# Twelve of twenty filler blocks as seven-product pairs ahead of a gated-DeltaNet recurrence

## The chip, the cores and the metric

The kernel runs on one core of one Trainium2 chip. The metric is the device time of one execution in microseconds. The engines are TensorE (PE in the profile), VectorE (DVE), ScalarE (ACT), GpSimd (POOL) and SyncE (SP), which issues most DMAs. They run side by side, each in its own order, and wait for each other on semaphores.

## The reference

One block of a streaming encoder on x of 1024 frames by 1024 channels, all float32:

```
proj = x @ w_in                      # 4872 columns: attention q/k/v, DeltaNet q/k/v,
                                     # beta, decay, output gate z, two branch gates
A = banded attention with rotary and sinks (chunks of 64 frames, window 2 chunks)
q, k, v = silu(causal_conv4(dqkv)); q, k l2-normalized
# chunked gated delta rule, per head (4 heads of 128), chunk of 64:
m_low = strict_lower((k*beta) k^T * decay);  t_inv = inverse(I + m_low)
u = t_inv (v*beta);  w = t_inv (k*beta*exp(g));  a = (q k^T) * decay
v_new = u - w state;  o = (q*exp(g)) state + a v_new
state = state*exp(g_last) + (k*exp(g_last - g))^T v_new        # scan over chunks
B = rmsnorm(o) * silu(z)
y = sigmoid(gateA) * (A @ wbA) + sigmoid(gateB) * (B @ wbB)
x = LN(alpha*x + y @ w_out);  x = LN(alpha*x + relu(x @ w_up)^2 @ w_down)
```

The change touches the input projection, the recurrence and their order, and no formula.

## The kernel before, in words

Every large product of two float32 matrices is made of three matmuls on operands split into a high and a low part (hi*hi, hi*lo, lo*hi), each 128 by 128 by 512 columns. The input projection has 37 blocks of 128 output columns. A plain block is 2 halves of 512 frames x 8 contraction tiles x 3 = 48 such matmuls. Two blocks taken together can be made with seven products of half size instead of eight (the scheme of Strassen and Winograd, `in7`, L2040): 7 x 4 x 3 = 84 matmuls for two blocks instead of 96. POOL makes the sums of the weights (`in_sums`), ACT the high parts (`in_hi`) and copies of partial results (`in_snap`), DVE the low parts (`in_lo`) and the additions (`combine_in`).

Block 0 is made plainly, blocks 1 to 16 in `N_IP = 8` pairs, and the last 20 blocks (4 of z, 16 of gates) plainly. The first of these 20 is made directly behind the pairs. The other 19 are **fillers**: PE puts their matmuls (L2118) one by one between the small products of the recurrence, in numbers written out by hand. Their weights come through two ring slots, split by POOL (`split_ring`, L774 and L777). A finished half block is copied out by ACT (`evac_half`, L980) and stored to DRAM (`park`), from where it is read back.

The recurrence goes over 8 tiles of 128 frames (two chunks each), all four heads at once. It is pipelined by hand: step t works on **t**, the scan and the attention of tile t; on **a** = t+1, the inverse of that tile's triangular matrix (five levels `a_y`, `a_u`, PE and DVE in turn, L2185, L1567, L1573, L1578); and on **n** = t+2, transposes, norms and decays of that tile (`a_grow`, `a_trk`, `a_trq`, `a_trv`, `a_d`, `a_norm`, `a_kd`, `a_vb`, `a_ee`). The functions named `step` of PE, DVE and ACT give each engine's order. For tile t and chunk c the scan is `b_ks` (state read, L2243), `b_x` (DVE), `b_vn` (product with the inverse, L2253), ACT's copy to `vn`, `b_ds` (state product, L2263), `b_state` (DVE). The attention is `b_scores`, `b_max`, `b_exps`, `b_prob`, `b_pt`, `b_pv`. The output is `b_o`, `b_osq` (squares on ACT), `b_on` (DVE: twelve small dependent operations for an inverse root, then two scalings), `b_ont`, `b_yd`. `a_norm` holds a second root of the same kind for q and k. Small DVE operations in `chain` wait each for the one before.

POOL makes the rotary products of tile t+1 once the second score product of tile t is done (`rope`), and one or two weight splits per step. SP loads each tile's data a step or more ahead. Steps -2 and -1 fill the pipeline; PE's numbers of fillers per place are

```
full = [12, 2, 6, 0, 3, 12, 0, 1, 0, 11, 2, 9, 11, 2, 11, 0, 2, 4, 1]   # then the rest up to 96
```

for the steps of tiles 0 to 6, so 96 fillers (two blocks) per step, and 96 in tile 7's step. Behind the recurrence come the branch projections (L2370), w_out, and the FFN.

Of the kernel before, what the change touches and what calls it, by code (L numbers as in the profile page):

```python
# [29 lines left out]
ALU = mybir.AluOpType  # L30
# [26 lines left out]
N_STD = 3  # L57
PIECES = ("A11", "A12", "S3", "A22", "S1", "S2", "S4")
# [12 lines left out]
N_IP = 8  # L71
# [58 lines left out]
def hybrid_block(nc, A, out):  # L130
    with ExitStack() as ctx:
# [53 lines left out]
        vn = workb("vn", 512, [P, NH, P])  # L185
# [23 lines left out]
        dqs = worka("dqs", 512, [P, NH, P])  # L209
        dd, eml, emu, em0 = [worka(name, 256, [P, NH, CH]) for name in ("dd", "eml", "emu", "em0")]  # L210
# [289 lines left out]
        def _(sp):  # L500
# [21 lines left out]
            def load_dv(t):  # L522
                sp.dma_start(dv[:, :, :], park[2 * NH:3 * NH, :, bass.ds(PAD + t * P, P)].rearrange("b p s -> p b s")).then_inc(dv_in, 16)
# [8 lines left out]
            def load_qk(t):  # L532

                if isinstance(t, int) and t == 0:
                    for h in range(2):
                        sp.wait_ge(ub_out[h], 16 * (B_DZ - N_DN))
# [82 lines left out]
            load_v(NT - 1)
            load_dz(NT - 1)  # L620
# [145 lines left out]
        def _(pool):  # L766
# [120 lines left out]
        def _(act):  # L887
# [53 lines left out]
            def in_snap(n, i):  # L941
# [59 lines left out]
            for n in range(N_IP):  # L1001
# [6 lines left out]
                if n == N_IP - 1:  # L1008
# [10 lines left out]
                if n == N_IP - 1:  # L1019
# [12 lines left out]
            in_snap(N_IP - 1, 3)  # L1032
            store_pair(N_IP - 1)
            act.sem_inc(uni_out, 4 * N_IP)
# [4 lines left out]
            for h in range(2):  # L1039
                evac_half(B_DZ, h, 2 * (B_DZ % 2) + h, ACT.Silu)  # L1040
# [55 lines left out]
            def b_vn(t, c):  # L1096
                act.wait_ge(vn_mm, 2 * t + (c + 1))
                r = slice(c * CH, (c + 1) * CH)
                cp(vn[r, :, :], (C0h, C1h)[c][r]).then_inc(vn_ok, 1)
# [8 lines left out]
            def step(t, a, n, p, fill):  # L1108

                if a is not None: a_t1(a, p)  # L1110
                if t is not None: b_vn(t, 0)
                if t is not None: b_exps(t, 0)
                if t is not None: b_pt(t, 0)
                fill(0)
                if t is not None: b_ya(t, 0)
                if t is not None: b_vn(t, 1)
                if n is not None: a_scalars(n, 1 - p)
# [1443 lines left out]
```

## Time and profile before

| | |
|---|---|
| time, median of 3 runs | 1417.92 us (1417.14 to 1417.92) |
| the profiled execution | span 1415.8 us from its first to its last instruction; some 2 us lie around it |
| PE busy | 1401.8 us (99%) |
| DVE, ACT, POOL busy | 978.8, 577.9, 277.7 us |
| pairs (blocks 1 to 16) | to 188.0 us |
| block 17, steps -2 and -1 | 188.0 to 251.4 us |
| steps of tiles 0 to 6 | 251.4 to 570.1 us |
| step of tile 7 | 570.1 to 605.9 us |

The profile gives each instruction's start and duration, and for idle time of an engine the instruction that ended it. Matmuls are pipelined: a row's duration overlaps the next one's, so the cost of one is the distance between starts.

### The profile page before, as it was taken

Reading aid. Unit: us, or ns where it says so; the run is one execution under the profiler, and the core shown is the slowest. Engines: PE = TensorE matmul, PEld = TensorE weight load, DVE = VectorE, ACT = ScalarE, POOL = GpSimd, SP = SyncE. Lnnn points to the kernel's source line nnn. Section 1 sums busy time; section 2 is a strip of 40 time slices with the busy share of each in tenths; the row PEclk is TensorE's granted clock in tenths of the full one; section 3 lists DMA queues with packets and bytes.
Section 4 is the critical chain, followed back from the end, with each engine's and each line's share of the span. In section 5 each row is a group of like instructions: output and inputs, shape, how many; then the busy total and the mean of one; then the engine's idle time right before and its main releaser. Section 6 shows DMA issues by size and latency. Waiting matters only on the chain.

```text
span 1415.8 us, 22360 instructions
## 1 busy us (share of the span) xinstructions
PE 1401.8 (99%) x8502; PEld 1154.4 (82%) x8502; DVE 978.8 (69%) x1792; ACT 577.9 (41%) x1258; POOL 277.7 (20%) x301
## 2 busy tenths in 40 slices
PE   9999999999999999999999999999999999999997
PEld 8788887888888888778888888888888888888885
DVE  7999844666666665364528797666674777777778
ACT  5655532323332332342203355555544544444540
POOL 4332234423333243323910000000000000000002
PEclk9999999999999999999999999999999999999999
DMA  6233362443244422234442144433345875555422
GB/s 212 90 119 114 109 194 86 122 119 105 75 114 113 120 64 88 72 113 161 166 176 90 60 165 162 164 147 131 137 158 192 324 238 180 163 165 187 126 69 119
DMA packets 114134, 195.01 MB, mean 138 GB/s; under 512 B 27696, under 2 KB 59632, under 8 KB 111728
## 3 DMA queue, kind: packets, MB, share of 16 engines
q1 hardware_dynamic: 105104, 174.21, 37.2%
q10 hardware_dynamic: 8928, 19.40, 3.6%
q8 instruction: 68, 1.11, 0.3%
q14 instruction: 34, 0.28, 0.1%
HBM read 135.84 MB, written 57.74 MB: 137 GB/s over the span
## 4 chain that ended last, share of the span: by engine, by line
PE 93%; DVE 5%; DMA 1%; issue 1%; SPq 0%; ACT 0%; ACTq 0%; DVEq 0%
PE ps L2118 16%; PE ps L2495 6%; PE ps L2493 6%; PE ps L2494 6%; PE ps L2476 6%; PE ps L2477 6%; PE ps L2478 6%; PE ps L2185 4%; PE ps L2003 4%; PE ps L2004 4%; PE ps L2005 4%; PE ps L2063 3%; PE ps L2065 3%; PE ps L2064 3%; PE ps L2374 2%; PE ps L2370 2%
## 5 line engine op out<-in xcount | busy, mean ns | idle before, releaser
L2493 PE MATMUL ps<-thi,shi 128*128 128x512 f32 x416 | 161.8, 389 | 0.0
L2494 PE MATMUL ps<-tlow,shi 128*128 128x512 f32 x416 | 161.8, 389 | 0.0
L2495 PE MATMUL ps<-thi,slow 128*128 128x512 f32 x416 | 161.8, 389 | 0.0
L878 POOL TENSOR_TENSOR zt<-zt,ln2gb 128x256 f32<-128x256 f32 x4 | 3.4, 851 | 691.6 <-ACT zt L1329 691.6
L2118 PE MATMUL ps<-xh,ring2l 128*128 128x512 f32 x304 | 124.5, 410 | 0.0
L2118 PE MATMUL ps<-xl,ring2h 128*128 128x512 f32 x304 | 123.6, 407 | 0.0
L2118 PE MATMUL ps<-xh,ring2h 128*128 128x512 f32 x304 | 122.3, 402 | 0.0
L888 ACT ACTIVATE thi<-b 128x512 fp32r<-128x512 f32 x104 | 65.5, 630 | 106.5 <-PE ps L2495 106.0
L1887 DVE TENSOR_TENSOR tlow<-b,thi 128x512 fp32r<-128x512 f32 x104 | 71.8, 690 | 51.8 <-ACT thi L888 51.7
L2494 PEld LDWEIGHTS ps<-tlow,shi 128*128 128x128 f32 x416 | 78.1, 188 | 16.3
L2495 PEld LDWEIGHTS ps<-thi,slow 128*128 128x128 f32 x416 | 78.1, 188 | 16.2
L2493 PEld LDWEIGHTS ps<-thi,shi 128*128 128x128 f32 x416 | 78.1, 188 | 16.1
L777 POOL TENSOR_TENSOR ring2l<-raw,ring2h 128x256 fp32r<-128x256 f32 x112 | 89.6, 831 | 2.2
L1880 DVE TENSOR_TENSOR slow<-sraw,shi 128x512 fp32r<-128x512 f32 x104 | 71.3, 686 | 22.5 <-ACT shi L888 21.7
L888 ACT ACTIVATE shi<-sraw 128x512 fp32r<-128x512 f32 x104 | 65.0, 625 | 33.5 <-DMA zt<-xpark 17.6
L774 POOL CAST ring2h<-raw 128x1024 fp32r<-128x1024 f32 x28 | 31.3, 1117 | 228.1 <-PE ps L2118 138.2
L2118 PEld LDWEIGHTS ps<-xl,ring2h 128*128 128x128 f32 x304 | 57.1, 188 | 12.3 <-issue 0.6
L2118 PEld LDWEIGHTS ps<-xh,ring2l 128*128 128x128 f32 x304 | 57.1, 188 | 12.0 <-issue 0.6
L2118 PEld LDWEIGHTS ps<-xh,ring2h 128*128 128x128 f32 x304 | 57.2, 188 | 11.4 <-issue 0.2
L1397 DVE SCALAR_TENSOR_TENSOR cacc<-cb,convw,cacc 128x1024 f32<-128x1024 f32 x36 | 51.6, 1435 | 2.1 <-ACT cacc L959 1.3
L980 ACT ACTIVATE ub<-ps 128x512 f32<-128x512 f32 x40 | 24.0, 601 | 67.5 <-PE ps L2118 65.7
L2003 PE MATMUL ps<-slh,mg 128*128 128x512 f32 x128 | 50.0, 390 | 0.0
(442 smaller groups left out, 3636.9 us busy)
## 6 DMA issues: line engine op xcount, KB each, us to landing
raw<-in_wblk SPq DMA_DIRECT2D x55, 512.0 KB, 3.6
sraw<-hpark SPq DMA_DIRECT2D x104, 256.0 KB, 2.8
hpark<-hq SPq DMA_DIRECT2D x16, 1024.0 KB, 4.6
b<-in_wblk SPq DMA_DIRECT2D x64, 256.0 KB, 3.6
wraw<-in_wblk SPq DMA_DIRECT2D x30, 512.0 KB, 4.0
hpark<-hq SPq DMA_DIRECT2D x16, 768.0 KB, 5.0
park<-ub ACTq DMA_DIRECT2D x40, 256.0 KB, 2.1
park<-cacc ACTq DMA_DIRECT2D x12, 512.0 KB, 3.3
```

The source lines that it names most:

```text
L777: ins = pool.tensor_tensor(lo[:, k:k + 2, :], src[:, k:k + 2, :], hi[:, k:k + 2, :].bitcast(F32), ALU.subtract)
L888: cp = lambda o_, i_: act.activation(o_, i_, ACT.Copy)
L1880: tt(slow[s][:, :], sraw[s][:, :], shi[s][:, :].bitcast(F32), ALU.subtract).then_inc(lsl_ok if last else sl_ok, 1)
L1887: tt(tlow[m][:, :], src[:, :], thi[m][:, :].bitcast(F32), ALU.subtract).then_inc(ltl_ok if last else tl_ok, 1)
L2003: mm(outp, lh, rh, start=start, stop=False)
L2118: ins = mm(ps[h][:, :], w, x_, start=(r == 0), stop=(r == 23))
L2476: mm(outp, hi[:, k, :], bh_, start=first, stop=False, skip_group_check=True)
L2477: mm(outp, hi[:, k, :], bl_, start=False, stop=False, skip_group_check=True)
L2478: last = mm(outp, lo[:, k, :], bh_, start=False, stop=final, skip_group_check=True)
L2493: mm(outp, shi[s][:, ts], thi[m][:, :], start=first, stop=False, skip_group_check=True)
L2494: mm(outp, shi[s][:, ts], tlow[m][:, :], start=False, stop=False, skip_group_check=True)
L2495: return mm(outp, slow[s][:, ts], thi[m][:, :], start=False, stop=final, skip_group_check=True)
```

## The change

`N_IP` goes from 8 to 14, so blocks 1 to 28 are made in pairs; blocks 29 to 36 (`LATE` = 29 on), all gates, remain as fillers, 8 x 48 = 384 matmuls. `FILLS` says how many go to each of 31 places of each of the ten steps: 50, 35, 30, 41, 27, 31, 33, 39, 33 and 65 for steps -2 to 7. The loops over tiles are written out. Each engine's order within a step is new. The computation of the decay rates and its three small products move into the eighth and the last pair. The clearing of buffers moves behind DVE's work of step -2. `vn` becomes two buffers, each holding one chunk's rows with zeros in the other half, and the state product reads all 128 rows. POOL splits one block in steps 0, 1, 3, 4 and 6, behind the rotary work.

```diff
-N_IP = 8
+N_IP = 14
+LATE = 2 * N_IP + 1
+FILLS = [
+    [0, 0, 6, 0, 1, 0, 0, 0, 0, 0, 0, 0, 0, 1, 0, 1, 0, 2, 2, 0, 0, 0, 13, 1, 2, 0, 0, 21, 0, 0, 0],
+    [0, 0, 0, 3, 0, 3, 0, 0, 3, 0, 2, 3, 2, 1, 0, 0, 3, 0, 0, 1, 0, 3, 0, 0, 0, 0, 0, 0, 5, 1, 5],
+    [2, 1, 0, 0, 0, 2, 0, 4, 1, 0, 0, 0, 0, 0, 0, 0, 0, 0, 3, 0, 6, 0, 0, 2, 5, 0, 0, 0, 0, 4, 0],
+    [4, 2, 1, 0, 0, 2, 0, 4, 1, 0, 0, 0, 0, 0, 0, 0, 0, 0, 3, 0, 6, 0, 0, 4, 3, 0, 0, 0, 0, 11, 0],
+    [0, 0, 0, 0, 0, 2, 0, 4, 1, 0, 0, 0, 0, 0, 0, 0, 0, 0, 2, 0, 3, 0, 0, 2, 9, 0, 0, 0, 0, 4, 0],
...
+    [0, 3, 0, 0, 4, 0, 8, 0, 2, 3, 0, 3, 0, 0, 1, 1, 1, 0, 1, 10, 0, 19, 0, 0, 0, 0, 0, 9, 0, 0, 0],
+]
@@ POOL
-            split_ring(N_IP + 1, 1)
-            split_ring(10, 0)
             rope(0)
-            split_ring(10, 1)
-            split_ring(11, 0)
-            with pool.Fori(0, NT - 1) as t:
+            split_ring((LATE + 2) // 2, 1)
+            behind = {0: LATE + 3, 1: LATE + 4, 3: LATE + 5, 4: LATE + 6, 6: LATE + 7}
+            for t in range(NT - 1):
                 rope(t + 1)
-                split_ring(t + 11, 1)
-                split_ring(t + 12, 0)
+                if t in behind:
+                    split_ring(behind[t] // 2, behind[t] % 2)
@@ DVE
+            def clear():
...
+                dve.memset(st[:, :, :], 0.0).then_inc(s_ok, 1)
+                dve.memset(vn0[CH:P, :, :], 0.0)
+                dve.memset(vn1[0:CH, :, :], 0.0)
+                dve.memset(qb[:, :, :, :], 0.0).then_inc(init_ok, 1)
+            step(-2)
+            clear()
+            for s in range(-1, NT):
+                step(s)
@@ PE: state product
-                r = slice(c * CH, (c + 1) * CH)
...
-                    last = mm(C1h[:, h, :], kdec[p][r, h, :], vn[r, h, :], start=True, stop=True)
+                    last = mm(C1h[:, h, :], kdec[p][:, h, :], vnz[c][:, h, :], start=True, stop=True)
@@ PE: state read and solve
-                    if not (isinstance(t, int) and t == NT - 1):
-                        pe.wait_ge(vb_ok, t + 2)          # in b_ks, c == 0
+                    if t < NT - 1:
+                        pe.wait_ge(vb_ok, t + 2)          # in b_vn, c == 0
@@ PE: order of a step (fills between the lines left out)
+                b_ks(t, 0); b_scores(t, 0); a_kk(a); a_kq(a); b_vn(t, 0); a_t1(a); b_ds(t, 0); a_y(a, 1); b_ks(t, 1)
+                b_pt(t, 0); a_ut(a, 1); a_u(a, 1); b_vn(t, 1); a_y(a, 2); b_pv(t, 0); a_u(a, 2); a_ut(a, 2)
+                b_scores(t, 1); b_ds(t, 1); a_y(a, 3); b_o(t, 0); b_o(t, 1); a_u(a, 3); a_ut(a, 3); a_grow(n); a_y(a, 4)
+                b_pt(t, 1); a_u(a, 4); a_ut(a, 4); a_trk(n); b_ont(t); a_trq(n); a_y(a, 5); b_pv(t, 1); a_u(a, 5); a_trv(n)
+            step(-2, FILLS[0])
+            pe.wait_ge(init_ok, 1)
+            for s in range(-1, NT):
+                step(s, FILLS[s + 2])
@@ DVE: order of a step
+                b_x(t, 0); a_m(a); b_max(t, 0); a_att(a); b_state(t, 0); b_prob(t, 0); a_ys(a, 1); b_x(t, 1); a_tb(a, 1)
+                a_r(a, 1); a_ys(a, 2); a_r(a, 2); a_tb(a, 2); a_qeg(a); b_max(t, 1); a_ys(a, 3); b_state(t, 1); a_r(a, 3)
+                a_tb(a, 3); b_prob(t, 1); a_d(n); a_ys(a, 4); b_on(t); a_r(a, 4); a_tb(a, 4); a_em(n); b_yd(t); a_ys(a, 5)
+                a_kd(n); a_norm(n); a_r(a, 5); a_ee(n); a_vb(n)
```

The last two parts are shortened: in the kernel each call stands on a line with a condition that its tile exists. In ACT's new order the squares of k and q come behind the copy of a filler's first finished half; in SP's, the second weight block of a step is gone.

## Rows read from the trace of the kernel before

**Rows 1.** The page, part 1: busy time, share of the span, instructions by engine.
```profile
PE 1401.8 (99%) x8502; PEld 1154.4 (82%) x8502; DVE 978.8 (69%) x1792; ACT 577.9 (41%) x1258; POOL 277.7 (20%) x301
```

**Rows 2.** Busy us by stage: span, PE, PEld, DVE, ACT, POOL, clock, DMA.
```profile
53.00:188.02 135.02, 135.02 (x597) 111.60 (x596) 121.20 (x143) 69.67 (x100) 39.69 (x30) 1.00 0.30 110
188.02:251.40 63.38, 62.85 (x515) 50.02 (x514) 27.99 (x75) 20.05 (x58) 26.19 (x33) 1.00 0.47 146
...
297.60:343.80 46.20, 46.20 (x486) 37.60 (x485) 30.67 (x89) 14.78 (x65) 15.68 (x20) 1.00 0.37 104
```

**Rows 3.** Order of time, PE: first state product of tiles 0, 1, 7; branch projection.
```profile
251.45 1.05 PE L2243 MATMUL ps<-st,kq 128*128 128x128 f32 x8
...
297.61 1.05 PE L2243 MATMUL ps<-st,kq 128*128 128x128 f32 x8
...
570.09 1.05 PE L2243 MATMUL ps<-st,kq 128*128 128x128 f32 x8
...
605.95 0.42 PE L2370 MATMUL ps<-yh,ring2h 128*128 128x512 f32 x1
```

**Rows 4.** Order of time, PE: first product of two neighbouring pairs.
```profile
111.86 0.39 PE L2063 MATMUL ps<-xh,ipA11h 128*128 128x512 f32 x1
...
130.90 0.39 PE L2063 MATMUL ps<-xh,ipA11h 128*128 128x512 f32 x1
```

**Rows 5.** Order of time, PE, within the step of tile 1 (and just before).
```profile
296.70 0.39 PE L2118 MATMUL ps<-xh,ring2l 128*128 128x512 f32 x1
...
298.50 1.06 PE L2215 MATMUL ps<-kr,qb 128*128 128x128 f32 x8
...
303.99 0.64 PE L2185 MATMUL ps<-rinv,mm 64*64 64x64 f32 x15
304.57 0.50 PE L2118 MATMUL ps<-xh,ring2l 128*128 128x512 f32 x1
304.90 0.39 PE L2118 MATMUL ps<-xh,ring2h 128*128 128x512 f32 x1
...
305.46 1.16 PE L2263 MATMUL ps<-vn,kdec 64*128 64x128 f32 x8
306.55 0.50 PE L2118 MATMUL ps<-xh,ring2l 128*128 128x512 f32 x1
...
330.89 0.60 PE L2126 MATMUL ps<-cst,pr 128*128 128x128 f32 x4
331.33 0.60 PE L2126 MATMUL ps<-cst,dqk 128*128 128x128 f32 x4
```

**Rows 6.** Order of time, DVE, same step: beside POOL, and the output norm's root.
```profile
316.09 1.20 DVE L1589 TENSOR_SCALAR nmx<-mx 128x4 f32<-128x4 f32 x1
...
322.69 1.26 DVE L1516 TENSOR_TENSOR emu<-dd,cst 128x256 f32<-128x256 f32 x1
...
327.50 0.16 DVE L1617 SCALAR_TENSOR_TENSOR ssb<-ssb,rqs 128x4 f32<-128x4 f32 x1 [0.43 <-ACT osb L1105]
...
329.68 0.16 DVE L1620 TENSOR_TENSOR nwu<-nwu,rqs 128x4 f32<-128x4 f32 x1
```

**Rows 7.** Order of time, POOL, same step: rotary work, then a weight split.
```profile
315.99 1.27 POOL L821 TENSOR_TENSOR qsw<-qsw,cs 128x512 f32<-128x512 f32 x1
...
319.01 2.92 POOL L830 TENSOR_TENSOR qb<-qraw,qsw 64x256 f32<-64x256 f32 x4
322.35 1.32 POOL L774 CAST ring2h<-raw 128x1024 fp32r<-128x1024 f32 x1 [0.42 <-POOL qb L830]
323.75 3.34 POOL L777 TENSOR_TENSOR ring2l<-raw,ring2h 128x256 fp32r<-128x256 f32 x4
```

**Rows 8.** Order of time, ACT's queue and DVE behind the last pair.
```profile
189.64 2.24 ACTq L973 DMA_DIRECT2D park<-cb  x4
...
197.32 0.91 DVE L1501 MEMSET qb<- 128x1024 f32 x1 [4.38 <-DMA park<-cb]
198.29 0.48 DVE L1502 MEMSET st<- 128x512 f32 x1
```

More of the change, by code:

```diff
@@ L970, in store_pair @@
                 act.wait_ge(cs_ok, 4 * n + 4)
+                if 2 * n + 1 >= B_DZ and 2 * n + 1 < B_GATE:
+                    for block in range(2):
+                        c = cb[2 * (n % 2) + block][:, 3:3 + S]
+                        act.activation(c, c, ACT.Silu).then_inc(silu_ok, 1)
+                    act.wait_ge(silu_ok, N_DN + 2 * n + 3 - B_DZ)
                 for block in range(2):
@@ L1038, in _ @@
             act.activation(G[:, :, G_SDE:G_SDO + NH], G[:, :, G_SDE:G_SDO + NH], ACT.Exp).then_inc(g_dif, 1)
-            for h in range(2):
-                evac_half(B_DZ, h, 2 * (B_DZ % 2) + h, ACT.Silu)
+            in_snap(N_IP - 1, 3)
+            store_pair(N_IP - 1)
+            act.sem_inc(uni_out, 4 * N_IP)
             def a_scalars(t, p):
@@ L1106, in b_osq, with late_half, step @@
                 ins.then_inc(osq_ok, 1)
-            def step(t, a, n, p, fill):
-                if a is not None: a_t1(a, p)
+            def late_half(i):
+                b, h = LATE + i // 2, i % 2
+                evac_half(b, h, h + 2 if b == LATE else h, ACT.Copy)
+            def step(s):
+                t = s if s >= 0 else None
+                a = s + 1 if 0 <= s + 1 < NT else None
+                n = s + 2 if s + 2 < NT else None
+                p, q = s % 2, 1 - s % 2
+                first, last = sum(map(sum, FILLS[:s + 2])) // 24, sum(map(sum, FILLS[:s + 3])) // 24
@@ L1144, in _ @@
-            step(None, 0, 1, 0, z_fill)
-            for i in range(NT // 2 - 1):
-                step(2 * i, 2 * i + 1, 2 * i + 2, 1, gate_fill(2 * i))
-                step(2 * i + 1, 2 * i + 2, 2 * i + 3, 0, gate_fill(2 * i + 1))
-            step(NT - 2, NT - 1, None, 1, gate_fill(NT - 2))
-            step(NT - 1, None, None, 0, lambda i: gate_fill(NT - 1)(i) if i < 3 else None)
+                if t is not None: b_ya(t, 1)
+                for i in range(first + 1, min(last, 2 * (B_BR - LATE) - 1)):
+                    late_half(i)
@@ L1152, in _ @@
+            for s in range(-2, NT):
+                step(s)
             act.wait_ge(yd_ok, NT)
@@ new lines, in _, with fill @@
+            pe.sem_inc(uni_mm, 4 * N_IP)
+            late = {"units": 0}
+            def fill(count):
+                for _ in range(count):
+                    j, r = divmod(late["units"], 48)
+                    h, r = divmod(r, 24)
+                    k, i = divmod(r, 3)
+                    b = LATE + j
+                    s_ = b % 2
+                    if h == 0 and r == 0:
+                        pe.wait_ge(w_ready, b + 1)
+                    if r == 0 and j == 0:
+                        if h == 0:
+                            pe.wait_ge(cs_ok, 4 * (N_IP - 1) + 1)
+                        else:
+                            pe.wait_ge(snap_ok, 4 * (N_IP - 1) + 4)
+                    elif r == 0:
+                        pe.wait_ge(uni_out, 2 * b + h + 1 - (4 if j == 1 else 2))
+                    sl = slice(h * HALF, (h + 1) * HALF)
+                    w = (ring2h, ring2h, ring2l)[i][s_][:, k, :]
+                    x_ = (xh, xl, xh)[i][:, k, sl]
+                    ins = mm(ps[2 + h if j == 0 else h][:, :], w, x_, start=(r == 0), stop=(r == 23))
+                    if r == 23:
+                        ins.then_inc(uni_mm, 1)
+                    late["units"] += 1
@@ L2270, in b_o @@
                 for h in range(NH):
-                    last = mm((O0h, C0h)[c][other, h, :], att[p][r, h, :], vn[r, h, :], start=False, stop=(h == NH - 1), skip_group_check=True)
+                    last = mm((O0h, C0h)[c][other, h, :], att[p][r, h, :], vnz[c][r, h, :], start=False, stop=(h == NH - 1), skip_group_check=True)
                 last.then_inc(o_mm, 1)
```

390 lines of the change are left out of this document (171 added, 219 removed), and 4 rows, old and new, of the table FILLS.

## The prediction

> **What bounds the kernel now.** I began with the page. The tensor engine (PE) is busy 1401.8 of 1415.8 us [rows 1]. So the end is set by what PE has to do, and each instruction taken from PE is a gain as long as nothing else becomes late. The second view was the busy time by stage, with the granted clock at 1.00 of 2.4 GHz in each [rows 2]. In the seven-product pairs before the change DVE is busy 121 of 135 us, since the convolutions run there too. In one step of the recurrence (46.2 us) PE is busy throughout, DVE 30.7 us, ACT 14.8 and POOL 15.7. So DVE would have 15 us to spare in a step. The third view was PE's order of time, where a step's start can be read at the first state product: tile 0 at 251.45, tile 1 at 297.61, tile 7 at 570.09, and the branch projection begins at 605.95 [rows 3]. A pair takes 130.90 - 111.86 = 19.04 us for 84 products, 0.2267 each [rows 4]. A filler costs (297.61 - 296.70)/4 = 0.2275 us [rows 3, 5]. The busy time of 0.39 us that a row names overlaps its neighbour and isn't the cost.
>
> The profiled span is 1415.8 us, the median of the timed runs 1417.9; 2.1 us lie around the span. I sum on the trace and add the difference to 1417.9.
>
> **Stage 1, the pairs.** Six more of them: 6 x 19.04 = +114.2 us. They have no convolution from the eighth on, so DVE has room for the chain of small gate operations that moves into one of them (some 27 operations of 0.2 us). The Silu of four blocks moves to ACT there, which runs nothing long. If that cover were missing, the next pair would start late by what DVE has left over, up to 5.4 us once; I take 0. The three small gate products (0.6 us) only change place.
>
> **Stage 2, from the last pair to tile 0's first state product.** Before: 251.45 - 188.02 = 63.4 us, with 192 plain products. After: 87 fillers. I follow the order. The last sum waits for ACT's copy (0.6) and DVE's addition (0.7); then ACT issues four stores, 2.24 us [rows 8], and only then copies the scalars of tile 0. That is 4.2 us, and the 13 fillers put ahead of the row transposes fill 3.1 (13 x 0.2275, and 0.1 for the change): PE idles 1.1 us. Then 37 fillers (8.4), three more groups of transposes (331.33 - 330.89 = 0.44 each, 1.3) [rows 5] and the changes between them, to 14.8. Now the clearing of buffers sits behind DVE's last work of tile 0, no longer ahead of it: V scaled 0.7, memsets of the state 0.48 and of qb 0.91 [rows 8], and two new ones on half the partitions, which no row shows. Nearest is the state's 0.48, so 0.3 to 0.5 each; I take 0.4. PE waits for the clearing with no filler behind the last transposes: 3.3 us idle, to 18.1. Step -1 has 17 groups of 16 small products (304.57 - 303.99 = 0.58 each at most, 0.56 on average, 9.5), four of transposes (1.8), 35 fillers (8.0) and 12 changes between them (0.15, 1.8): 21.1. [rows 5] With two fillers of step 0 (0.5) and the gate products (0.6) it makes 40.3 us, -23.1. The wait for the pairs' stores, which held qb up by 4.4 us [rows 8], is met over 10 us after the stores are issued and costs nothing.
>
> **Stage 3, tiles 0 to 6.** Before: 570.09 - 251.45 = 318.6 us with 660 fillers (150.2), so 168.4 of other PE work, 24.1 per step. Now 232 fillers, 52.8 us. A filler that follows a small group starts a slower pair: 304.57 to 304.90 is 0.33, against 0.23 [rows 5]. There were 14 groups of fillers per step, now about 10: -0.7 per step. The state products on 64 rows took 306.55 - 305.46 = 1.09 us, those on 128 rows 298.50 - 297.61 = 0.89 where the same shape follows [rows 3, 5]. Widening them with zeros is worth 0 to 0.4 per step; I take 0.2, as the neighbours are mixed. So PE's floor is 168.4 - 6.3 + 52.8 = 214.9 us, 30.7 per step.
>
> DVE is now as near. Its 30.7 us hold 4.3 us in which seven operations were stretched while POOL ran: nmx took 1.20 us beside POOL's rotary products, where such small operations alone take 0.16, and emu 1.26 beside a weight split [rows 6, 7]. The row of nmx ends at 317.29, and POOL's product of qsw, begun before it, at 317.26: nmx was held until POOL let go. Add 1.1 us of gaps between dependent small operations: DVE needs 27.5 us of its own. Waits that the order can't fill, by walking through it with these durations: for the first state update 0.4, the second state read 0.5, the first tb 0.3, the second ys 1.1, together 2.3. Then POOL. Rotary work starts at each second score product, where DVE comes with mx, nmx, sdf: +1.8 as now. It runs about 7.2 us (its second product begins at 315.99, the last ends at 321.93, and the first is as long as the second) [rows 7] and meets the softmax scaling: +0.6. That makes 27.5 + 2.3 + 2.4 = 32.2 us a step for steps 2 and 5, which have no weight split. In steps 0, 3 and 4 a split of 4.4 us (cast 1.3, four subtractions) follows the rotary work directly, when DVE is in the twelve dependent operations of the output norm, which alone take 2.4 us (327.50 to 329.85) [rows 6]. Five of them can each be held to the end of a POOL instruction (+0.4 to +0.65): +2.4, so 34.6. In step 1 the split waits for its ring slot and meets less: 33.3. Step 6 prepares no further tile, which takes 6 us from DVE, so PE sets it: 29.2. Sum: 2 x 32.2 + 3 x 34.6 + 33.3 + 29.2 = 230.7, -87.9. PE idles 16 us of it.
>
> Bounds of this term: PE's floor 214.9 below. Above, the waits are 4.2 us as in the same walk without any stretch, and each step is stretched as now, 4.3: 36 per step, 245.
>
> The Trainium skill, "SBUF — State Buffer", section "Who interferes with whom", says that a DVE instruction with two SBUF inputs and a GpSimd one that reads SBUF exclude each other, and the second waits for the whole of the first. The rows of nmx and emu agree. [...]
>
> **Stage 4, tile 7.** Before 605.95 - 570.09 = 35.9 with 96 fillers (21.8), so 14.0 of other work. After: 65 fillers, 14.8, less 0.8 for changes: 28.0, -7.9. The chain of tile 7 alone (two state passes, squares, norm, transposes, gating) is about 20 us, so it is covered.
>
> **Moved at no cost.** SP's loads are re-ordered and twelve weight loads go to the pairs. Each tile's loads are still issued over 10 us ahead of use, and none waits behind a queue that PE waits for; POOL's rotary work loses two splits per step and gets room. The wait for the next tile's scaled V moves from the first state read to the solve behind it. It lies on PE, with score and Gram products ahead of it now, and costs only where DVE is late anyway (counted above). If it were later than the solve's other operand, the state chain behind it would wait too.
>
> **Sum.** 114.2 - 23.1 - 87.9 - 7.9 = -4.7 us: 1413.2 us. Check from the other side: 72 products fewer, -16.4; fewer changes and wider products -7.1; idle PE +4.4 and +16; less 1 us of idle before: about -4.
>
> **Rivals.**
> A, DVE becomes the bound in earnest (slower). Place: the output norm and the next tile's q/k norm, some 25 dependent small operations per step, beside POOL. A step then takes 36 us, stage 3 is 6 x 36 + 29.2 = 245: +9.8 us, 1427.7. Stage 3 breaks even at 235.4 us, steps of (235.4 - 29.2)/6 = 34.4; it decides, slower by 0.2%, from 34.8 on. For: DVE would be over 90% busy in a step, and the granularity of the stretches is POOL's, 0.6 to 1.3 us. Against: only 5 splits are left in 8 steps instead of two per step.
> B, PE stays the bound. The stretches fall into DVE's waits, stage 3 is 218 (the floor and 3 us): -17.4, 1400.5. For: after an operation is held, the next wait is often shorter; PE has all its other work to do. Against: rows show DVE's second half of a step (output norm, key decay, q/k norm, scaled V) as one chain without waits.
> C, the gain is spent: steps of 34.2 us on average, stage 3 is 234.4: -1.0, 1416.9. For and against it stands what does for the forecast, with a stretch of 1 us more per step.
> D, the tensor clock falls. The granted clock is 1.00 in every stage of before [rows 2], and all of PE's idle time together is 14 us. The new pause at the clearing is 3.3 us. If the clock fell to 1.2 GHz there for step -1, its 35 fillers would cost 0.2275 more each: +8, 1421. The Trainium skill, "TensorE: Matmul & The Clock Gate", section "HAM oscillation — how this bites in real kernels", warns of just such pauses; no row of this trace shows whether this one is long enough.
>
> **Chances.** Forecast 0.31, A 0.25, B 0.22, C 0.19, D 0.03. 0.2% is 2.8 us, about what a measurement of this kernel can tell from no change. Faster: forecast and B, 0.53. Same: C, 0.19. Slower: A and D, 0.28. The range runs from a little below B to A: 1399 to 1429. The forecast's own range is 1409 to 1416.
>
> **What would show it.** Pairs of 19.0 us through the fourteenth, without a DVE wait. A pause of PE of about 3 us behind tile 0's last transposes, ended by a memset of qb. First state products 31 to 35 us apart, with the steps of tiles 2 and 5 shorter by 2 us than those of 0, 3 and 4. PE idle ahead of the solve (b_vn of the first chunk), the Gram products and the output transposes, ended by DVE. Newton's small operations at 0.6 us and more beside weight splits: none did so before. The state products in the group now 0.9 us instead of 1.09. The forecast is wrong if DVE idles over 5 us in a step while PE idles too (then it is the dependence between them and not DVE's load), or if the pairs wait.

## The result, and the profile after

| | us |
|---|---|
| before, median (lowest to highest) | 1417.92 (1417.14 to 1417.94) |
| after, median (lowest to highest) | 1432.05 (1428.98 to 1435.67) |
| ratio, 95% interval | 1.0102 [1.0085, 1.0119]: slower |
| forecast, range | 1413.2, 1399 to 1429 |
| profiled execution: time, span, mean clock | 1435.67, 1433.9, 0.988 (before: span 1415.8, clock 0.998) |

The forecast had the wrong sign, and the time lies 3 us outside the range. The profiled execution is the slowest of the four; its stages are compared with each other, and medians are used for what a part is worth. The four executions of after have spans of 1427.0, 1429.2, 1431.1 and 1433.9 us at mean clocks of 0.993, 0.991, 0.991 and 0.988: the lower the granted clock, the longer.

Part 1 of the page, kernel after. It answers to [rows 1]:
```profile
PE 1392.7 (97%) x8430; PEld 1154.0 (80%) x8430; DVE 1024.1 (71%) x1860; ACT 600.7 (42%) x1300; POOL 257.4 (18%) x265
```
The 72 products fewer are there (8502 to 8430), and PE is busy 9 us less in a span 18 us longer. So PE now waits, 41 us instead of 14, and part of what it does runs slowly.

Windows by stage, kernel after (columns as in [rows 2]): from within the eighth pair to the end of the last; from there to tile 0's first state product (of the state read, `b_ks`); tiles 0 to 6; tile 7; from the branch projection to the end:
```profile
172.56:307.22 134.66, 132.34 (x578) 108.87 (x578) 56.27 (x104) 48.28 (x82) 35.19 (x29) 0.99 0.34 118
307.22:350.57 43.35, 38.55 (x392) 29.32 (x391) 22.56 (x67) 9.78 (x45) 14.83 (x19) 0.92 0.47 132
350.57:593.02 242.45, 223.68 (x2934) 187.92 (x2932) 208.64 (x603) 89.06 (x417) 71.61 (x88) 0.97 0.34 90
593.02:622.31 29.29, 27.20 (x170) 21.98 (x166) 15.44 (x49) 10.69 (x45) 7.68 (x10) 1.00 0.24 82
622.31:1433.90 811.59, 801.00 (x3556) 663.27 (x3556) 567.33 (x895) 346.44 (x573) 68.22 (x78) 0.99 0.45 156
```
The pairs end 4.4 us later than forecast (307.22; 188.0 + 114.2 and 0.6 for the gate products is 302.8): from start to start the tenth takes 22.91 us, the eleventh 19.65, the others 19.04. Stage 2 is 43.35, without the gate products 39.7 in the forecast: +3.7. Stage 3 is 242.45 and not 230.7: +11.8. Stage 4 is 29.3 and not 28.0: +1.3. The rest is 811.6 and was 809.9: +1.7. Together 22.8 us, the whole distance of 1433.9 from the forecast span of 1411.1. The granted clock, 1.00 in all stages of before, is below 1.00 in four of the five.

PE, kernel after, order of time. First the pause at the clearing of buffers and a filler's product behind it; then tile 0's first state product, the pause ahead of tile 0's output transposes and what follows it:
```profile
320.90 0.60 PE L2122 MATMUL ps<-cst,dv 128*128 128x128 f32 x4
325.17 0.69 PE L2159 MATMUL ps<-dqk 128*64 128x64 f32 x16 [3.67 <-DVE qb L1512]
...
326.67 0.63 PE L2114 MATMUL ps<-xh,ring2h 128*128 128x512 f32 x1
...
350.57 1.05 PE L2242 MATMUL ps<-st,kq 128*128 128x128 f32 x8
...
376.99 0.39 PE L2114 MATMUL ps<-xh,ring2l 128*128 128x512 f32 x1
379.96 0.66 PE L2122 MATMUL ps<-cst,osb 128*128 128x128 f32 x4 [2.58 <-DVE osb L1632]
380.45 0.60 PE L2122 MATMUL ps<-cst,dqs 128*128 128x128 f32 x4
380.98 1.06 PE L2181 MATMUL ps<-rinv,mm 64*64 64x64 f32 x16
...
386.67 1.05 PE L2242 MATMUL ps<-st,kq 128*128 128x128 f32 x8
```
The step of tile 0 is 386.67 - 350.57 = 36.1 us. The same pause comes in the steps of tiles 3, 4 and 6 (2.81, 2.66, 2.62 us). Behind each of them groups of 16 small products take 1.06 to 1.12 us, and plain ones behind the pause at 325 take 0.63 (0.64 and 0.39 before, [rows 5]): PE runs at 1.2 GHz for some us. The seven steps are 36.1, 34.6, 31.8, 37.5, 36.1, 33.0 and 33.4 us; the forecast was 34.6, 33.3, 32.2, 34.6, 34.6, 32.2 and 29.2.

Windows, kernel after, around the pauses at 325 and 380:
```profile
324.00:328.00 4.00, 2.55 (x35) 1.66 (x35) 3.05 (x6) 0.00 (x0) 2.73 (x3) 0.81 1.19 285
328.00:332.00 4.00, 3.89 (x36) 2.92 (x37) 0.48 (x3) 0.50 (x2) 3.84 (x7) 0.50 0.14 35
332.00:336.00 4.00, 4.00 (x54) 2.75 (x55) 1.33 (x4) 0.00 (x0) 3.63 (x5) 0.84 0.44 110
...
382.00:390.00 8.00, 8.00 (x79) 6.41 (x79) 6.21 (x27) 1.22 (x5) 0.00 (x0) 0.84 0.57 150
```
A granted clock of 0.50 is 1.2 GHz throughout, 0.84 is part of the window at it.

The branch projection begins behind a wait too, and behind it the clock falls once more:
```profile
622.31 0.47 PE L2373 MATMUL ps<-yh,ring2h 128*128 128x512 f32 x1 [2.10 <-ACT yh L896]
```

DVE in the same step, order of time: a small operation beside the rotary work, then the first six of the output norm, and one behind them:
```profile
366.82 1.20 DVE L1599 TENSOR_SCALAR nmx<-mx 128x4 f32<-128x4 f32 x1
...
373.62 0.80 DVE L1627 SCALAR_TENSOR_TENSOR ssb<-ssb,rqs 128x4 f32<-128x4 f32 x1
374.44 0.17 DVE L1628 TENSOR_SCALAR ssb<-ssb 128x4 f32<-128x4 f32 x1
374.65 0.58 DVE L1355 TENSOR_SCALAR nwv<-ssb 128x4 int32<-128x4 int32 x1
375.26 0.66 DVE L1356 TENSOR_SCALAR nwu<-nwv 128x4 int32<-128x4 int32 x1
375.95 0.65 DVE L1357 TENSOR_TENSOR nwv<-nwu 128x4 f32<-128x4 f32 x1
376.64 0.66 DVE L1358 TENSOR_TENSOR nwv<-nwv,ssb 128x4 f32<-128x4 f32 x1
377.34 0.16 DVE L1359 SCALAR_TENSOR_TENSOR nwv<-nwv 128x4 f32<-128x4 f32 x1
```
and POOL beside it:
```profile
373.36 1.04 POOL L784 CAST ring2h<-raw 128x1024 fp32r<-128x1024 f32 x1 [0.29 <-POOL qb L840]
374.47 2.81 POOL L787 TENSOR_TENSOR ring2l<-raw,ring2h 128x256 fp32r<-128x256 f32 x4
```
Five of the twelve dependent operations take 0.58 to 0.80 us instead of 0.16 ([rows 6]). The last held one ends at 377.30, the last subtraction of POOL at 377.28. From there they take 0.16 again. Three of the five read two inputs from SBUF: ssb with rqs, nwu with itself, nwv with ssb. Of such operations the Trainium skill, "SBUF — State Buffer", section "Who interferes with whom", says that they contend with a GpSimd instruction that reads SBUF. The trace agrees, with 377.30 and 377.28. The two others, nwv<-ssb and nwu<-nwv, have one such input and were held as well (0.58 and 0.66 us). The same holds for nmx in [rows 6]: it has one input, so it shows that an operation is held, but not the rule on two inputs. One small operation with one input did pass: in the step of tile 1 before, DVE's `reciprocal` took 0.18 us at 325.31, in the midst of POOL's subtractions. The norm's root took 2.3 us before and takes 4.9 here. The mechanism of the forecast is there, with five held operations as counted.

ACT and PE in the tenth pair, order of time. ACT stores the z blocks of the ninth pair here:
```profile
215.81 1.28 ACT L984 ACT_TABLE_LOAD   x1
217.11 2.01 ACT L984 ACTIVATE cb<-cb 128x1024 f32<-128x1024 f32 x2
219.15 1.81 ACTq L988 DMA_DIRECT2D park<-cb  x4
221.34 0.63 ACT L896 ACTIVATE ipS1h<-ipS1r 128x512 fp32r<-128x512 f32 x1 [2.23 <-POOL s4raw L809]
```
```profile
222.60 0.47 PE L2060 MATMUL ps<-ithT,ipS3h 128*128 128x512 f32 x1 [2.00 <-ACT cb L896]
...
224.45 0.63 PE L2061 MATMUL ps<-itlT,ipS3h 128*128 128x512 f32 x1
```
The Silu of z (table load, two activations, four stores: 5.1 us on ACT) stands ahead of the cast of S1 and of the copy that frees a sum; PE waits 2.00 us, and then also here products of 0.63 us follow, from 224.45 on.

### The profile page after: what moved, and what is told of

It is laid out like the page before. It is cut to its first block, busy times and chain, and to the rows that moved or that the text cites. A ratio compares the mean times of both kernels' runs of the same rounds, so it can differ in the third digit from the quotient of the medians.

```text
span 1433.9 us, 22065 instructions
## 1 busy us (share of the span) xinstructions
PE 1392.7 (97%) x8430; PEld 1154.0 (80%) x8430; DVE 1024.1 (71%) x1860; ACT 600.7 (42%) x1300; POOL 257.4 (18%) x265
## 4 chain that ended last, share of the span: by engine, by line
PE 85%; DVE 11%; issue 1%; DMA 1%; ACT 1%; SPq 0%; ACTq 0%; DVEq 0%
PE ps L2498 6%; PE ps L2497 6%; PE ps L2496 6%; PE ps L2060 6%; PE ps L2479 6%; PE ps L2480 6%; PE ps L2481 6%; PE ps L2062 6%; PE ps L2061 6%; PE ps L2114 5%; PE ps L2000 4%; PE ps L2001 4%; PE ps L2002 4%; PE ps L2181 3%; PE ps L2373 2%; PE ps L2374 2%
## 5 line engine op out<-in xcount | busy, mean ns | idle before, releaser
L2114 PE MATMUL ps<-xh,ring2h 128*128 128x512 f32 x128 | 54.7, 427 | 0.0
L2114 PE MATMUL ps<-xh,ring2l 128*128 128x512 f32 x128 | 54.6, 426 | 0.0
L896 ACT ACTIVATE cb<-ps 128x512 f32<-128x512 f32 x58 | 34.3, 591 | 47.1 <-PE ps L2062 41.4
L2114 PE MATMUL ps<-xl,ring2h 128*128 128x512 f32 x128 | 53.9, 421 | 0.0
L1423 DVE TENSOR_TENSOR cb<-cb,ps 128x512 f32<-128x512 f32 x56 | 38.1, 680 | 18.5 <-PE ps L2062 12.2
L787 POOL TENSOR_TENSOR ring2l<-raw,ring2h 128x256 fp32r<-128x256 f32 x64 | 50.4, 818 | 1.3
L2000 PE MATMUL ps<-slh,mg 128*128 128x512 f32 x128 | 50.1, 391 | 0.2 <-issue 0.2
L2002 PE MATMUL ps<-slh,mg 128*128 128x512 f32 x128 | 49.9, 390 | 0.0
L2001 PE MATMUL ps<-sll,mg 128*128 128x512 f32 x128 | 49.9, 389 | 0.0
L1416 DVE TENSOR_TENSOR ipS1l<-ipS1r,ipS1h 128x512 fp32r<-128x512 f32 x14 | 21.1, 1510 | 37.2 <-POOL ipS2r L805 23.9
```

Source lines behind the costliest of these rows:

```text
L896: cp = lambda o_, i_: act.activation(o_, i_, ACT.Copy)
L2000: mm(outp, lh, rh, start=start, stop=False)
L2001: mm(outp, lh, rl, start=False, stop=False)
L2002: return mm(outp, ll, rh, start=False, stop=stop)
L2114: ins = mm(ps[2 + h if j == 0 else h][:, :], w, x_, start=(r == 0), stop=(r == 23))
```

## The experiments

All are compared with the same kernel before, 1417.7 to 1418.1 us beside them. Four change one thing in the kernel after.

**e1, PE kept busy in the pauses.**
```diff
+                if t in (0, 3, 4, 6):
+                    pe.wait_ge(pt_ok, 2 * t + 2)
+                    for _ in range(11):
+                        mm(T0[:, :], xh[:, 0, 0:P], xh[:, 0, 0:HALF], start=True, stop=True)
                 ...            # ahead of b_ont's transposes; 16 such products ahead of the wait for the clearing
```


> PE is given 11 needless products ahead of the output transposes in the steps of tiles 0, 3, 4 and 6 (2.5 us each at full clock), and 16 ahead of the wait for the cleared buffers (3.6 us). They go to banks that are written anew behind them. Theory 1 (the pause itself costs little more than its length, the clock that falls behind it costs the rest): the granted clock stays at 1.00 there, step -1 is shorter by some 2 us and each of the four steps by 1 to 2 us, the whole 6 to 10 us below the changed kernel, 1422 to 1426 us. Rival (DVE alone sets the steps, the low clock lies under its slack): the clock stays up and the steps keep their 36.1, 37.5, 36.1 and 33.4 us; no change within 2 us, 1430 to 1434.


Measured: 1427.39 us, ratio 1.0070 [1.0053, 1.0086], 4.7 us less than after. The same windows:
```profile
328.00:332.00 4.00, 4.00 (x71) 3.01 (x71) 1.27 (x3) 0.00 (x0) 3.63 (x6) 1.00 0.00 0
...
382.00:390.00 8.00, 8.00 (x105) 7.14 (x104) 7.18 (x24) 2.46 (x11) 0.00 (x0) 1.00 0.68 161
```
The clock stays up, though the added products do nothing. Steps of tiles 0, 3, 4 and 6 are 0.7 to 1.4 us shorter (35.2, 36.8, 35.3, 31.9). The gain lies below the expected one, and e1 takes part of it back itself: in three of the four steps the added products begin late and last beyond the pause. In the step of tile 0 the norm's output is ready at 376.08, and its transposes begin at 376.73:
```profile
374.11 2.78 PE L2342 MATMUL ps<-xh 128*128 128x512 f32 x11 [0.55 <-ACT prt L896]
376.73 0.60 PE L2122 MATMUL ps<-cst,osb 128*128 128x128 f32 x4
```
The overrun is 0.65, 0.91 and 0.79 us in steps 0, 3 and 4, and 0.05 in step 6. So 4.7 us is a low figure for what the covered falls cost; a comparison of the steps that doesn't depend on it stands below, with e2.

**e2, the splits later.** In the recurrence POOL begins each weight split behind DVE's scaled V of the tile after next, behind the output norm.
```diff
                 rope(t + 1)
                 if t in behind:
+                    if t < NT - 2:
+                        pool.wait_ge(vb_ok, t + 3)
+                    else:
+                        pool.wait_ge(yd_ok, t + 1)
                     split_ring(behind[t] // 2, behind[t] % 2)
```


> POOL starts each weight split of the recurrence only when DVE has scaled the next tile's V, so at the end of the step instead of beside the output norm. Theory 2 (four to six small operations of the output norm, held to the end of a POOL instruction each, make DVE late and open PE's pause of 2.6 to 2.8 us): the norm takes 2.4 us in all steps, the pause shrinks to under 1 us and the clock does not fall, steps of tiles 0, 3, 4 and 6 become 32 to 34 us, the whole 8 to 14 us below the changed kernel, 1418 to 1424. What is left of the stretch moves to the first score product's small operations, 1 us a step. Rival (the dependence between DVE and PE sets the steps, the split only happens to lie there): pauses before the output transposes stay above 2 us, and the time within 3 us of the changed kernel.


Measured: 1416.61 us, ratio 0.9990 [0.9981, 1.0000], 15.4 us less than after. The norm and the split, order of time of DVE and of POOL, and the window of tiles 0 to 6:
```profile
371.89 0.15 DVE L1631 SCALAR_TENSOR_TENSOR ssb<-ssb,rqs 128x4 f32<-128x4 f32 x1
...
374.07 0.16 DVE L1634 TENSOR_TENSOR nwu<-nwu,rqs 128x4 f32<-128x4 f32 x1
```
```profile
383.39 1.04 POOL L784 CAST ring2h<-raw 128x1024 fp32r<-128x1024 f32 x1 [12.04 <-DVE vb L1557]
```
```profile
348.84:574.59 225.75, 217.97 (x2933) 183.98 (x2932) 198.51 (x603) 88.55 (x417) 68.91 (x84) 1.00 0.36 95
```
The same work on PE and DVE takes 16.7 us less in stage 3 only because POOL's splits lie elsewhere (most of that of tile 6's step now falls into tile 7's: 84 instead of 88 instructions of POOL here). The pauses ahead of the output transposes are gone (one of 0.3 us is left), and with them the falls of the clock in this stage. This is the main cause. The four long steps, cut where DVE ends the norm's output (`osb`), in us:

| step | start to `osb`: after, e1, e2 | `osb` to the next step: after, e1, e2 |
|---|---|---|
| 0 | 29.34, 29.35, 26.82 | 6.76, 5.83, 5.50 |
| 3 | 30.25, 30.26, 27.74 | 7.23, 6.49, 5.72 |
| 4 | 29.62, 29.66, 27.07 | 6.47, 5.68, 5.23 |
| 6 | 29.22, 29.25, 26.62 | 4.15, 2.69, 2.69 |

Up to the norm's output the split costs 2.5 to 2.6 us a step, with the clock up (e1) or not. Behind it the low clock costs 1.2 to 1.5; in step 6, where e1's products don't overrun, e1 and e2 agree. So per step the held operations are the larger part and the clock the smaller.

**e3, the Silu later.** The Silu and stores of pairs 8 and 9 go behind all of ACT's other work in the next pair.
```diff
-                if n > N_DN // 2:
+                if n > N_DN // 2 and n - 1 not in (8, 9):
                     store_pair(n - 1)
                 ...
+                if n - 1 in (8, 9):
+                    store_pair(n - 1)
```


> The Silu and the stores of the z pairs go to the end of ACT's work for the next pair, behind its copies of partial results. Theory 3: PE's waits on ACT in the pairs, 2.0 and 0.3 us, go, and with them the low clock behind the first; the pairs end 4 us earlier (303 instead of 307.2), the whole 3.5 to 5 us shorter, 1427 to 1429. Rival (the pairs wait on something that Silu only hides, the weight sums of POOL or the loads): another releaser takes its place and 2 us or less is won.


Measured: 1428.42 us, ratio 1.0069 [1.0052, 1.0086], 3.6 us less than after. No pause of PE is left in the pairs from the third on, each takes 19.04 us, and tile 0's first state product comes at 345.14 instead of 350.57.

**e4, the clearing earlier**: `clear()` one step up, ahead of tile 0's q/k norm on DVE.


> The clearing of the buffers goes ahead of the q/k norm of tile 0 on DVE, instead of behind all its work of step -2. Theory: PE's wait of 3.7 us there becomes under 1 us and the clock does not fall; tile 0's matrix then waits for the norm, so that a wait of 2 us or so opens ahead of the first small products; 2 to 4 us are won, 1428 to 1430. Rival: the wait only moves behind the Gram products, with the same low clock, and the time stays within 1 us.


Measured: 1436.52 us, ratio 1.0128 [1.0111, 1.0145], 4.5 us more than after: a miss. DVE, POOL and PE in order of time:
```profile
322.52 1.23 DVE L1360 SCALAR_TENSOR_TENSOR nwy<-nwt,nwy 128x8 f32<-128x8 f32 x1
323.79 1.20 DVE L1361 SCALAR_TENSOR_TENSOR nwt<-nwy 128x8 f32<-128x8 f32 x1
```
```profile
322.46 1.27 POOL L830 TENSOR_TENSOR qraw<-qraw,cs 128x512 f32<-128x512 f32 x1 [9.69 <-DMA ksw<-park]
```
```profile
331.67 1.12 PE L2174 MATMUL ps<-cst,tb 64*64 64x64 f32 x16 [6.92 <-DVE tb L1568]
```
The wait isn't removed, it moves behind the solve's first operand and grows. In after POOL's rotary work of tile 0 is released by the end of the clearing, behind the norm, and begins at 325.27; here it begins at 322.46, as soon as its load has landed. The norm's chain, which ran alone before at 0.17 us an operation, now runs beside it: two operations take 1.2 us and five 0.5 to 0.64. What is released counts, as well as what is waited for.

The next four build on e2, and the last two on b1.

**e5, state products on 64 rows** (as before the change):
```diff
-                    last = mm(C1h[:, h, :], kdec[p][:, h, :], vnz[c][:, h, :], start=True, stop=True)
+                    last = mm(C1h[:, h, :], kdec[p][c * CH:(c + 1) * CH, h, :], vnz[c][c * CH:(c + 1) * CH, h, :], start=True, stop=True)
```


> On top of the later splits, the state products read 64 rows again (the zero halves are left unread). Theory 4 (the widening is worth what the shapes beside it are worth, 0 to 0.4 us a step): 0 to 3 us slower than the kernel with later splits alone, 1416.6 to 1419.5. Rival (reading rows of zeros costs): 1 us or more faster.


Measured: 1418.69 us, ratio 1.0008 [0.9999, 1.0018], 2.1 us more than e2; tiles 0 to 6 take 227.3 instead of 225.75, 0.23 per step. A group of eight takes 1.09 us from its start to the next group's on 64 rows, and with the zeros 0.98 where small products follow and 0.81 where a filler does. Zeros on the other rows are worth it, by about the 0.2 taken; that the medians differ by 2.1 is within what executions of one kernel differ here.

**e6, no rotary work for tiles 1 to 7.** POOL only signals; q and k of the attention are then not rotated there, and the attention's part of the output isn't the reference's.
```diff
+                if t > 0:
+                    pool.sem_inc(rope_mul, 4)
+                    pool.sem_inc(rope_low, 1)
+                    pool.sem_inc(rope_ok, 1)
+                    return
```


> On top of the later splits, POOL leaves out the rotary products and sums of tiles 1 to 7 (the attention reads tile 0's keys and zeros), so that in the steps POOL does nothing but five splits. By the prediction's sum, rotary work stretches DVE by 2.4 us a step where DVE sets the step: then steps of tiles 0 to 5 become 30.5 to 31.5 us instead of 31.9 to 33.5, and the whole is 6 to 12 us below the kernel with later splits, 1405 to 1411. Rival (the stretch lies in DVE's waits): steps change by under 0.7 us, 1412 to 1416.


Measured: 1403.99 us, ratio 0.9902 [0.9884, 0.9920], 12.6 us less than e2. Tiles 0 to 6:
```profile
348.88:561.22 212.34, 212.34 (x2934) 182.03 (x2932) 181.08 (x603) 88.27 (x417) 16.99 (x21) 1.00 0.38 101
```
PE doesn't wait once. So 212.3 us is its floor (214.9 in the forecast), and DVE beside the splits alone is busy 181.1/7 = 25.9 us a step, with 4.5 to spare. All that e2 loses against the floor, 13.4 us, goes with the rotary work. It stretches DVE by (198.5 - 181.1)/7 = 2.5 us a step, where the forecast had 2.4.

**e7, fillers into the two pauses.** 16 of tile 7's fillers go behind step -2's last transposes, where PE waits for the clearing, nine behind the last attention product, where it waits for the branch's input (2.10 us). Two splits are one step earlier for it.
```diff
-    [0, 0, 6, 0, 1, 0, 0, 0, 0, 0, 0, 0, 0, 1, 0, 1, 0, 2, 2, 0, 0, 0, 13, 1, 2, 0, 0, 21, 0, 0, 0],
+    [0, 0, 6, 0, 1, 0, 0, 0, 0, 0, 0, 0, 0, 1, 0, 1, 0, 2, 2, 0, 0, 0, 13, 1, 2, 0, 0, 21, 0, 0, 16],
...
-    [0, 3, 0, 0, 4, 0, 8, 0, 2, 3, 0, 3, 0, 0, 1, 1, 1, 0, 1, 10, 0, 19, 0, 0, 0, 0, 0, 9, 0, 0, 0],
+    [0, 3, 0, 0, 3, 0, 5, 0, 2, 2, 0, 3, 0, 0, 1, 1, 1, 0, 1, 5, 0, 13, 0, 0, 0, 0, 0, 0, 0, 0, 9],
...
-            behind = {0: LATE + 3, 1: LATE + 4, 3: LATE + 5, 4: LATE + 6, 6: LATE + 7}
+            behind = {0: LATE + 3, 1: LATE + 4, 2: LATE + 5, 4: LATE + 6, 5: LATE + 7}
```


> On top of the later splits: 16 fillers of tile 7's step go behind the last transposes of step -2, ahead of the wait for the cleared buffers, 9 others of tile 7's step go behind the last attention product, and two splits come a step earlier, since their blocks are now reached earlier. Theory 1 (pause and the low clock behind it): step -1 is 5 us shorter counted without the fillers, the 2.1 us wait ahead of the branch projection and the low clock behind it go (3 to 4 us); 7 to 9 us below the kernel with later splits, 1408 to 1410. Rival: the fillers taken from tile 7's step open pauses there, and blocks reached earlier wait for their splits: 3 us or less is won.


Measured: 1414.17 us (1411.66 to 1417.74), ratio 0.9979 [0.9970, 0.9988], 2.4 us less than e2: below what was expected. Both pauses are gone, but a wait of 0.89 us for tb and one of 1.77 us for ACT's copy of a filler come in step -1 and in tile 7's, and tiles 0 to 6 take 226.8 (+1.0). The profiled spans (1409.5 and 1415.1) differ by more than the medians: e7's is the shortest of its ten executions, at a mean clock of 0.998, and e2's is not, at 0.994. Where the mean clock is the same, 0.997, e2's spans are 1411.7 and 1412.0 and e7's 1411.5 to 1413.1. By these, what e7 won is mostly the falls of the clock, and the length of the two pauses came back elsewhere.

**b1, e7 and e3's edit together.** 


> As the one before, and with the Silu and the stores of the z pairs at the end of ACT's work for the next pair. If the parts add up: 15.4 (later splits), 7 to 9 (covered waits) and 3.6 us (Silu) below the changed kernel, 1404 to 1407, 0.8 to 1% faster than before. If the low clock behind one pause is shared with the next, less: 1407 to 1410.


Measured: 1410.69 us, ratio 0.9950 [0.9936, 0.9963]: 7 us less than before, 21 less than after, above the expected sum since e7 fell short. Tile 0's first state product comes at 344.10.

**b2, the rotary products earlier.** On b1: POOL's four rotary products start behind DVE's sdf of the first score product; only the sums stay behind the second.
```diff
-                    pool.wait_ge(sc_mm, 2 * t)
+                    pool.wait_ge(sm_ok, 2 * t - 1)
                 ...
                 pool.wait_ge(rope_mul, 4 * t + 4)
+                if t > 0:
+                    pool.wait_ge(sc_mm, 2 * t)
                 pool.tensor_tensor(kr[:, :], kraw[:, :], ksw[:, :], ALU.add)
```


> On the version that puts the weight splits later, the fillers into the two pauses and the Silu stores last (1410.7 us). One edit: POOL's four rotary products of tiles 1 to 7 start behind the first score product's maximum (sdf), no longer behind the second score product; only the sum for k and the four sums into qb stay there. Theory (two engines share a port; each small DVE operation waits for the POOL operation that runs): the first softmax scaling and nothing else meets the long products of 1.27 us, the second score product's mx, nmx and sdf meet sums of 0.6 to 0.84 us; steps 0.5 to 1.2 us shorter, 3 to 8 us in all, 1403 to 1408 us, and the wait of 0.9 us for ys shrinks. Rival (the rotary work costs the same wherever it lies, since POOL's busy time is what counts): within 2 us of 1410.7.


Measured: 1405.91 us (1405.28 to 1406.34), ratio 0.9913 [0.9900, 0.9927]: the fastest, 12 us less than before and 26 less than after. DVE in the step of tile 1, order of time, and the window of tiles 0 to 6:
```profile
392.83 0.65 DVE L1607 TENSOR_SCALAR nmx<-mx 128x4 f32<-128x4 f32 x1
393.52 0.16 DVE L1608 TENSOR_TENSOR sdf<-sink,mx 128x4 f32<-128x4 f32 x1
```
```profile
343.63:566.89 223.26, 217.97 (x2933) 184.40 (x2932) 194.33 (x603) 87.75 (x416) 72.24 (x88) 1.00 0.36 97
```
nmx is held by a sum, 0.65 us, and no longer by a product, 1.2. POOL's four sums beside it:
```profile
392.06 2.91 POOL L842 TENSOR_TENSOR qb<-qraw,qsw 64x256 f32<-64x256 f32 x4
```
The step waits of 0.9 us for ys are gone; in their place PE waits 0.3 to 0.85 us for pr, whose scaling now meets the products. Stage 3 is 3.5 us shorter than in b1 with the same work.

**b3, four fillers from behind the second score product to ahead of it.** On b1, meant to fill the 0.9 us wait for ys; they come from the place ahead of the second probability transposes.
```diff
-    [2, 1, 0, 0, 0, 2, 0, 4, 1, 0, 0, 0, 0, 0, 0, 0, 0, 0, 3, 0, 6, 0, 0, 2, 5, 0, 0, 0, 0, 4, 0],
+    [2, 1, 0, 0, 0, 2, 0, 4, 1, 0, 0, 4, 0, 0, 0, 0, 0, 0, 3, 0, 2, 0, 0, 2, 5, 0, 0, 0, 0, 4, 0],
...            # likewise in the other six steps
```


> On the same version. One edit: in steps 0 to 6, four fillers (three in step 2) move from ahead of the second probability transposes to ahead of the second u product, where PE waits 0.9 us for ys. Theory (DVE is the bound from there to the next tile's scaled V, it is busy without a gap from 394.8 to 412.5 us of that trace): the 0.9 us come back at the next wait for DVE (output transposes, ys of the fourth level), the time stays within 1.5 us of 1410.7. Rival (the order of fillers costs the pause): each of six steps is 0.9 us shorter, 1405 to 1406 us.


Measured: 1417.82 us, ratio 1.0000 [0.9991, 1.0009], 7.1 us more than b1; neither theory's number. My place was wrong: the wait of 0.9 us belongs to the third u product, behind the second scores, and these fillers stand ahead of the scores.
```profile
363.19 0.68 PE L2187 MATMUL ps<-ys,tb 64*64 64x64 f32 x16 [0.90 <-DVE ys L1583]
```
The wait is unchanged at 0.90, and the steps are longer by 1.1 us each, step 2 with its three fillers by 0.9, together 7.7 in the trace; the fillers themselves are 27 x 0.2275 = 6.1. That is an answer too: what PE does ahead of the second scores lies on the step's critical chain. By the rows it goes from the scores over DVE's mx, nmx, sdf and ys to the output norm. Their old place, behind the scores, was not on it, since nothing came back there.

## Why the prediction was wrong

- **The sum.** The step that failed is the term of stage 3, -87.9 in the forecast and -76.2 in the trace. Two things in it were wrong: step 6 was left without its split (4.2 us), and the clock was taken as 1.00 behind PE's pauses (4.0 us in steps 0, 3 and 4). The rest of the 11.8 is in step 3 (1.4 beyond the clock), step 1 (34.6 and not 33.3) and 0.9 of small sizes. The terms of stages 1 and 2 were off by 4.4 and 3.7. Stage 3 alone turns the sign, -4.7 + 11.8 = +7.1, and so would the two others together, -4.7 + 8.1 = +3.4.
- **Stage 3, step 6, "PE sets it": 29.2.** Wrong by 4.2. A weight split follows the rotary work in this step too, beside the output norm of tile 6, which was left out for this one step. e2, with the split later, gives 29.3. Of the 4.2, 2.6 are the held norm and 1.5 the clock behind it.
- **Stage 3, "+2.4" for a split beside the norm.** The count (five held operations) was right, and so was the price: 4.86 - 2.34 = 2.5 us on DVE, and the norm's output comes 2.5 to 2.6 us later than in e2. Without the low clock steps 0 and 4 would have been 34.8 us long each, against 34.6.
- **Stage 3, "the clock 1.00".** This is rival D, given 0.03 and tied to one place, the clearing. It holds there and behind the pauses ahead of the output transposes, which follow from the forecast's own 16 us of idle PE, but were nowhere listed one by one. By place, in the profiled execution, the slowest: 5.5 us in the four steps (the table at e2); 2.2 in step -1 (39.49 us from the first transposes behind the pairs to tile 0's first state product, 37.30 in e1); 1.6 in the tenth pair (22.91 us, and 21.33 in e1, where the same wait wasn't followed by a fall); 1.5 behind the branch projection's start (811.6, and 810.1 in e1). Together 10.8 of the 22.8 us, the largest single piece. The Trainium skill, "TensorE: Matmul & The Clock Gate", section "HAM oscillation — how this bites in real kernels", warns that PE's clock falls behind pauses. In that the trace agrees, with products at 0.63 us behind the pauses of 2.00, 3.67 and 2.10 us; the pauses in its example are longer than most of these.
- **Stage 3, steps 2 and 5, "32.2".** Measured 31.8 and 33.0, in total within 0.4 us. PE's floor, forecast 214.9, is 212.3 (e6).
- **Stage 1, "Silu at 0".** The price of 5.4 us stood in the sentence behind it, for DVE's work and not for this; the trace has 4.4, of which 1.6 are the clock, and e3 3.6 of the median. I looked at how busy ACT is in a pair and not at what stands behind the Silu on it: the cast and the copy for which PE waits next.
- **Stage 2.** The pause at the clearing was forecast at 3.3 us and is 3.67, ended by the memset of qb as said. Of the rest of the +3.7, 2.2 are step -1 at 1.2 GHz (clock 0.81, 0.50, 0.84 in three windows, 324 to 336). Rival D's +8 assumed all 35 fillers of that step at the slow level; the clock came back up within those 12 us. Where the last 1.1 went was not followed up.
- **Stage 4, tail.** The 2.10 us wait for ACT's copy ahead of the branch projection was not seen; the clock falls behind it too (0.79 from 622 to 630). e7 removes both.
- **Which rival?** A's direction and place (output norm beside POOL, 1427.7) fit best: stage 3 is 242.5 against its 245. A put the price on DVE's load. But in e2 DVE does the same work in 225.75 us: it is which operations meet, not how much DVE has to do. That is also the step behind the forecast's own "DVE is now as near".
- **Widening the state products, "0.2":** right, 0.23 per step (e5).
- **The forecast's own sign of being wrong**, DVE idle over 5 us in a step while PE idles too: DVE idles 5.0, 5.5 and 5.8 us in steps 1, 3 and 6 and 3.9 to 4.9 in the others. DVE was busy 86% of stage 3 (208.6 of 242.5) and never the 90% of rival A; the steps are set by the waits between DVE and PE as well as by DVE's work.

## What to carry to other kernels

Before a helper engine's block of work moves, or before the engine it slows loses its slack, list what lies beside it: a chain of small dependent operations pays one whole instruction of the helper per operation, and the same splits behind the chain left DVE busy 198.5 us in tiles 0 to 6 instead of 208.6. Moving the helper's work behind such a chain, with a wait on an engine that has just passed it, was worth 15 us here, and cutting its long products off it another 5. When PE no longer sets the end everywhere, count its pauses one by one: each costs its length and may cost a stretch of slow clock behind it, and work moved into it keeps the clock up, even where it brings back less of the length than it fills. Products that do nothing keep the clock up as well, but cost whatever they last beyond the pause.

## What was not expected of the hardware

- The clock fell behind pauses of 2.0 to 3.7 us, and behind the shorter of them not each time. Over the profiled executions, from the pairs to the start of the branch projection, all 18 pauses of 2.57 us and more were followed by a fall, and 8 of the 14 pauses of 2.0 to 2.1 us. The pause of 2.00 us in the pairs is the same in several kernels. Window 223 to 226 of e2 and of e7, which are alike up to there:
```profile
223.00:226.00 3.00, 3.00 (x8) 2.34 (x7) 1.50 (x3) 0.50 (x1) 0.00 (x0) 0.50 0.00 0
```
```profile
223.00:226.00 3.00, 3.00 (x15) 2.48 (x14) 1.89 (x4) 0.44 (x1) 0.41 (x1) 1.00 0.00 0
```
  PE made 8 products in one and 15 in the other, and the first transposes behind the pairs come 1.6 us later (311.01 and 309.39). Such falls spread the executions of one kernel: e2's spans go from 1411.7 us at a mean clock of 0.997 to 1417.1 at 0.993, while b2, with fewer long pauses, lies within 1.1 us. Differences of 2 us between such kernels need many executions. What decides whether a given pause lowers the clock was not found.
- A pause of 2.0 us (e2, in the pairs) was enough in some executions. Waits of 0.9 us, six in a row 33 us apart, were followed by no fall in e2's and b1's steps (the windows show 1.00), nor were the waits of 1.8 us in tile 7's step of e7, b1, b2 and b3.
- Zeros on the idle half of the rows made state products among full-height neighbours cheaper by 0.23 us a step of 16 products, and most where a filler follows them (0.81 instead of 1.09 us for eight).
